# A mixture-of-experts stage: first tiles prepared one expert ahead, extra rows gathered and turned once for up to four lots, VectorE's order and the record loads changed

## What is computed

```python
def expert_block(args):
    xb, e = args
    return (jax.nn.silu(xb @ exp_w1[e]) * (xb @ exp_w3[e])) @ exp_w2[e]
y_buf = lax.map(expert_block, (buf.reshape(n_blocks, MOE_BLOCK, d), block_expert))
y = y_buf.reshape(n_blocks * MOE_BLOCK, d)[dest] * gate_sorted[:, None].astype(h.dtype)
out = jnp.zeros((n_tok, d), h.dtype).at[tok_sorted].add(y)
```

## Time and profile before

| | |
|---|---|
| median of 3 executions | 3097.43 us (3096.23 to 3101.21) |
| profiled execution, its own time | 3096.11 us |
| its span | 3094.0 us |
| TensorE matmul busy | 2624.5 us (85%) |
| VectorE, ScalarE busy | 1299.9 us (42%), 1085.1 us (35%) |
| expert stage, first turning to last output product | 2160.2 to 3078.3 us |

### The profile page before, as it was taken

The page is one execution under the profiler, slowest core; times in us unless marked ns, Lnnn a source line. Parts: engine busy times, 40 slices in busy tenths (PEclk is TensorE's granted clock), DMA queues, the critical chain, the costliest instruction groups (busy, mean ns, idle before and its releaser), DMA issues. The chain is left out here.

```text
span 3094.0 us, 40387 instructions
## 1 busy us (share of the span) xinstructions
PE 2624.5 (85%) x12691; PEld 1750.5 (57%) x12692; DVE 1299.9 (42%) x2250; ACT 1085.1 (35%) x2054; POOL 680.2 (22%) x1351
## 2 busy tenths in 40 slices
PE   5879999999677959768999999970988898886997
PEld 1326444444445445447998899860655565554664
DVE  5634671221122314132344554420746565453664
ACT  2542111111221211212344545410645565443563
POOL 2640110000000000006145555553122212222221
PEclk8989999999888979875799999965999999998999
DMA  5972211110499696761011111103886798765793
GB/s 183 330 212 72 52 45 31 52 55 28 129 245 222 149 233 156 175 186 34 29 58 54 54 54 58 58 35 124 312 286 208 246 330 286 233 205 181 239 351 113
DMA packets 307937, 472.00 MB, mean 153 GB/s; under 512 B 26852, under 2 KB 195180, under 8 KB 300996
## 3 DMA queue, kind: packets, MB, share of 16 engines
q1 hardware_dynamic: 229815, 396.89, 40.3%
q0 software_dynamic: 18416, 44.58, 6.3%
q10 hardware_dynamic: 59616, 29.38, 3.5%
HBM read 370.64 MB, written 108.05 MB: 155 GB/s over the span
## 5 line engine op out<-in xcount | busy, mean ns | idle before, releaser
L798 PE MATMUL ps_proj<-sb_hT,sb_win 128*128 128x512 f32 x768 | 336.1, 597 | 7.6 <-DVE sb_rot L903 6.0
L798 PEld LDWEIGHTS ps_proj<-sb_hT,sb_win 128*128 128x128 f32 x768 | 145.7, 192 | 189.9 <-issue 183.0
L2191 PE MATMUL ps_byp<-sb_w,sb_gT 128*128 128x512 f32 x512 | 236.0, 604 | 3.9 <-ACT sb_gT L2006 3.9
L1917 DVE TENSOR_TENSOR sb_w1l<-sb_raw,sb_w1h 128x1024 fp32r<-128x1024 f32 x128 | 148.2, 1220 | 167.8 <-ACT sb_w1h L1978 167.8
L1407 POOL MEMSET sb_pr<- 128x1026 int32 x1 | 1.0, 958 | 907.7 <-POOLq L186 907.7
L1686 DVE CUSTOM_DVE_ANT_0 sb_pr<-ps_S,sb_mask 128x640 f32<-128x640 f32 x128 | 105.6, 825 | 216.8 <-PE ps_S L1535 216.6
L1204 DVE TENSOR_TENSOR sb_ab<-sb_ab,ps_prod 128x512 f32<-128x512 f32 x64 | 44.1, 689 | 356.1 <-ACT sb_ab L1180 356.1
L1555 PE MATMUL ps_O<-sb_v,sb_pt 128*128 128x64 f32 (+1 forms) x1280 | 176.0, 293 | 0.0
L1555 PEld LDWEIGHTS ps_O<-sb_v,sb_pt 128*128 128x128 f32 x1280 | 173.3, 214 | 0.0
L1614 ACT COPY sb_pt<-ps_PT 128x512 f32<-128x512 f32 x128 | 74.6, 583 | 275.5 <-PE ps_PT L1541 275.4
L1917 DVE TENSOR_TENSOR sb_w3l<-sb_raw,sb_w3h 128x1024 fp32r<-128x1024 f32 x128 | 150.5, 1217 | 0.7 <-ACT sb_w3h L1978 0.5
(11 more groups left out here) (291 smaller groups left out, 5658.3 us busy)
## 6 DMA issues: line engine op xcount, KB each, us to landing
sb_raw<-in_exp_w SPq DMA_DIRECT2D x64, 2048.0 KB, 17.5
sb_w<-in_exp_w SPq DMA_DIRECT2D x32, 2048.0 KB, 9.1
sb_ada<-in_ada_w SPq DMA_DIRECT2D x16, 1536.0 KB, 8.1
scr_filt<-sb_fout ACTq DMA_DIRECT2D x128, 128.0 KB, 4.5
sb_yh<-scr_filt SPq DMA_DIRECT2D x32, 512.0 KB, 11.2
scr_hy_y<-sb_sp SPq DMA_DIRECT2D x32, 512.0 KB
sb_yx<-scr_hy_y SPq DMA_DIRECT2D x32, 512.0 KB, 7.9
scr_hy_v<-sb_yx SPq DMA_DIRECT2D x64, 256.0 KB, 4.3
```

What stands on the lines that cost most here:

```text
L798: ins = pe.matmul(mp[:, (NQ + n) % 4, :], w[:, pc % 3, k, (ct % 2) * P:(ct % 2 + 1) * P], g.hT[:, k, c * 512:(c + 1) * 512], start=(k == 0 ...
L1917: ve.tensor_tensor(piece(low[m], part), piece(raw13[par][:, m], part), piece(high[m], part).bitcast(F32), ALU.subtract).then_inc(lo[m], 1)
L2191: ins = pe.matmul(yp[:, part, :], gT[:, f, :], w2[par][:, f, part * 512:(part + 1) * 512], start=(f == 0), stop=(f == FT - 1), skip_group_ ...
```

## The change

An expert's first lots and its main tile are now prepared during the expert ahead of it. All rows from 129 to 256 of an expert are gathered once (buffer xgx), turned once in 8 transposes between the two halves of the hidden products of the expert before (function ahead), and scaled into xfx, from which up to four lots take their 32 columns. The four lots are four copies of the lot's code, each inside a condition on r, the number of these lots; rows beyond 256 go through a second loop (far) with four more copies. Lots and main tiles have semaphores of their own. VectorE computes two of the four low parts of w1 before the gated product and two after it, and three of w3's after the output scaling; ScalarE no longer casts a part of w3 ahead of the gated copies. The records of all experts are loaded at the start of the stage by 18 transfers that ScalarE issues, two over 128 partitions and 16 over 32; each 8-byte record is an element of its own in them. SyncE loads only weights. TensorE waits, ahead of turning xg, for the first low part of the next w1.

```diff
@@ -1776,9 +1776,10 @@
     GR = P // LOT
     FQ = 2 * FH // GR
     DQ = D // GR
-    MANY = 1 + (T - P) // LOT
-    TILES = NE + 2 * T // LOT
-    SLOTS = TILES + MANY + 4
+    NL4 = P // LOT
+    LOTS = 2 * T // LOT
+    FAR = LOTS // NL4
+    R, FURTHER, LOTS_AT, GROUP_AT, FAR_AT = range(5)
...
-        rec = e.sb(st, "brec", [P, SLOTS, 2], I32)
...
+        rec = e.sb(st, "brec", [P, NE, 2], I32)
+        recx = e.sb(st, "lot_rows", [P, NE, 2], I32)
+        recl = e.sb(st, "lot_records", [P, NE, NL4, 2], I32)
...
+        xgx = e.sb(st, "xg_lots", [P, D])
+        xfx = e.sb(st, "bxf_lots", [P, KT, P])
...
-        def span(eng, ex):
-            many = eng.value_load(info[0:1, 0, bass.ds(ex, 1)], min_val=1, max_val=MANY)
-            lots = eng.value_load(info[0:1, 1, bass.ds(ex, 1)], min_val=0, max_val=TILES - NE)
-            return many, lots
-
-        def experts(eng, lot, main):
-            def one(ex, par, half, last):
-                many, lots = span(eng, ex)
-                with eng.If(many > 1):
-                    with eng.Fori(0, many - 1) as b:
-                        lot(lots + ex + b, lots + b, ex, par, half)
-                main(lots + ex + many - 1, ex, par, half, last, lots + many - 1)
+        def column(eng, which, ex, least, most):
+            return eng.value_load(info[0:1, which, bass.ds(ex, 1)], min_val=least, max_val=most)
+
+        def experts(eng, ahead, lot, far, main):
+            def one(ex, par, half, r, last):
+                def lots(x, j):
+                    lot(x + j, j, recl[:, bass.ds(ex, 1), j, :].rearrange("p a b -> p (a b)"), ex, par, half)
+                    if j + 1 < NL4:
+                        with eng.If(r > j + 1):
+                            lots(x, j + 1)
+                with eng.If(r > 0):
+                    x = column(eng, LOTS_AT, ex, 0, LOTS)
+                    lots(x, 0)
+                    further = column(eng, FURTHER, ex, 0, T // P - 1)
+                    with eng.If(further > 0):
+                        at = column(eng, FAR_AT, ex, 0, FAR)
+                        with eng.Fori(0, further) as f:
+                            far(at + f, ex, r, f)
+                            for j in range(NL4):
+                                lot(x + r + NL4 * f + j, j, recfl[:, j, :], ex, par, half)
+                after = None if last else column(eng, R, ex + 1, 0, NL4)
+                main(ex, par, half, last, after)
+                return after
             eng.wait_ge(cnt, 1)
+            first = column(eng, R, 0, 0, NL4)
+            ahead(0, first)
             with eng.Fori(0, NE // 2 - 1) as pair:
-                one(2 * pair, 0, pair, False)
-                one(2 * pair + 1, 1, pair, False)
-            one(NE - 2, 0, NE // 2 - 1, False)
-            one(NE - 1, 1, NE // 2 - 1, True)
-            return eng.value_load(info[0:1, 2, NE - 1:NE], min_val=0, max_val=TILES - NE) + NE
+                after = one(2 * pair, 0, pair, column(eng, R, 2 * pair, 0, NL4), False)
+                one(2 * pair + 1, 1, pair, after, False)
+            after = one(NE - 2, 0, NE // 2 - 1, column(eng, R, NE - 2, 0, NL4), False)
+            one(NE - 1, 1, NE // 2 - 1, after, True)
...
+        rows_of = g.table[0:NE * CAP, :].rearrange("(e t) c -> t e c", e=NE)
+        records = [(rec[:, :, :], rows_of[0:P]), (recx[:, :, :], rows_of[P:2 * P])]
+        for q in range(GR):
+            for j in range(NL4):
+                records.append((recl[q * LOT:(q + 1) * LOT, :, j, :], rows_of[P + j * LOT:P + (j + 1) * LOT]))
...
+            def ahead(ex, r):
+                with ve.If(r > 0):
+                    group = column(ve, GROUP_AT, ex, 0, NE)
+                    ve.wait_ge(ttx, group + 2)
+                    ve.sem_inc(passed_v, 1)
+                    scale_rows(xfx).then_inc(xx_v, 1)
...
-            def main(n, ex, par, half, last, lots):
...
+            def main(ex, par, half, last, after):
                 if not last:
-                    weights_low(ex + 1, 1 - par, 0, range(PARTS))
+                    ahead(ex + 1, after)
+                    weights_low(ex + 1, 1 - par, 0, (0, 1))
                 ve.wait_ge(sgd, ex + 1)
                 ve.wait_ge(hm[1], ex + 1)
                 for c in range(FT):
                     cs = slice(c * P, (c + 1) * P)
                     ve.tensor_tensor(sg[:, cs], sg[:, cs], hp[:, 1, cs], ALU.mult).then_inc(gd, 1)
-                scaled(n + 1)
                 if not last:
+                    scaled(ex + 1)
+                    weights_low(ex + 1, 1 - par, 0, (2,))
+                    rows_low(ex + 1)
+                    weights_low(ex + 1, 1 - par, 0, (3,))
                     weights_low(ex + 1, 1 - par, 1, (0,))
-                rows_low(n + 1)
-                if not last:
-                    weights_low(ex + 1, 1 - par, 1, range(1, PARTS))
-                ve.wait_ge(added, n + 1)
+                ve.wait_ge(added, ex + 1)
                 for part in range(2):
                     cs = slice(part * 512, (part + 1) * 512)
                     ve.wait_ge(ym, 2 * ex + part + 1)
-                    ins = ve.scalar_tensor_tensor(out=y[:, cs], in0=yp[:, part, :], scalar=gate(n), in1=g2[:, cs],
+                    ins = ve.scalar_tensor_tensor(out=y[:, cs], in0=yp[:, part, :], scalar=gate(ex), in1=g2[:, cs],
                                                   op0=ALU.mult, op1=ALU.mult)
                 ins.then_inc(y_ok, 1)
+                if not last:
+                    weights_low(ex + 1, 1 - par, 1, range(1, PARTS))
 
             scaled(0)
             rows_low(0)
             weights_low(0, 0, 0, range(PARTS))
             weights_low(0, 0, 1, range(PARTS))
             ve.wait_ge(ld, 16 * (1 + GR))
-            experts(ve, lot, main)
+            ve.wait_ge(rl, 16 * (len(records) - 1))
+            experts(ve, ahead, lot, far, main)
...
+            def main(ex, par, half, last, after):
                 def gated_copied(c):
                     act.wait_ge(gtt, 4 * ex + c + 1)
                     act.copy(gT[:, c, :], gp[:, c % 2, 0:P]).then_inc(gtc, 1)
                 act.wait_ge(hm[0], ex + 1)
                 act.activation(sg[:, :], hp[:, 0, :], ACT.Silu).then_inc(sgd, 1)
                 if not last:
+                    ahead(ex + 1, after)
                     weights_high(ex + 1, 1 - par, half + par, 0, range(PARTS))
-                act.wait_ge(hm[1], ex + 1)
-                if not last:
-                    weights_high(ex + 1, 1 - par, half + par, 1, (0,))
                 gated_copied(0)
                 gated_copied(1)
-                scaled(n + 1)
+                if not last:
+                    scaled(ex + 1)
                 gated_copied(2)
                 gated_copied(3)
-                rows_high(n + 1)
                 if not last:
-                    weights_high(ex + 1, 1 - par, half + par, 1, range(1, PARTS))
-
+                    rows_high(ex + 1)
+                    weights_high(ex + 1, 1 - par, half + par, 1, range(PARTS))
+
+            for c, (dst, src) in enumerate(records):
+                act.dma_start(dst, src).then_inc(rl if c else rl0, 16)
             scaled(0)
             rows_high(0)
             for m in range(2):
...
+            def gather(ex):
+                if not (isinstance(ex, int) and ex == 0):
+                    pool.wait_ge(tt, ex)
+                    pool.sem_inc(passed, 1)
+                gathered(xg, picked_in, gat, rec[:, bass.ds(ex, 1), 0:1].rearrange("p a b -> p (a b)"), 0, ex)
+
+            def gather_ahead(ex):
+                with pool.If(column(pool, R, ex, 0, NL4) > 0):
+                    group = column(pool, GROUP_AT, ex, 0, NE)
+                    pool.wait_ge(ttx, group + 1)
+                    pool.sem_inc(passed, 1)
+                    gathered(xgx, picked_x, gatx, recx[:, bass.ds(ex, 1), 0:1].rearrange("p a b -> p (a b)"), 1, group)
+
+            def ahead(ex, r):
+                gather_ahead(0)
+                gather(1)
+                gather_ahead(1)
+
...
+            def main(ex, par, half, last, after):
+                if not isinstance(ex, int):
+                    gather_ahead(ex + 2)
+                    gather(ex + 2)
+                pool.wait_ge(y_ok, ex + 2)
...
+            pool.wait_ge(rl0, 16)
             gather(0)
-            gather(1)
-            total = experts(pool, lot, main)
-            pool.wait_ge(scat, 16 * total)
-            pool.wait_ge(gat, 16 * (total + 2))
-            pool.sem_inc(passed, 1)
+            pool.wait_ge(rl, 16 * (len(records) - 1))
+            pool.sem_inc(ttx, 1)
+            experts(pool, ahead, lot, far, main)
...
-            def records(ex):
-                many, lots = span(sp, ex)
-                with sp.If(many > 1):
-                    with sp.Fori(0, many - 1) as b:
-                        sp.wait_ge(rl, 16 * (lots + ex + b + 1))
```

(48 more changed lines are left out.)

199 lines of the change are left out of this document (119 added, 80 removed).

## The result

The changed kernel takes 3344.56 us (median of 4 runs, 3338.85 to 3350.23) against 3099.32 us for the kernel before in the same runs: ratio 1.0787, 95% interval 1.0759 to 1.0816. It is 7.9% slower, where 1.0% was forecast.

A forecast was written before the change was run, and what follows sets the result against it. TensorE was taken to bound experts without lots, with excess time in experts with lots. 3096.1 - 55.8 - 6.2 - 15.5 + 26 + 84 = 3128.6, given as 3129 us, 1.0% slower; 8-in-10 range 3037 to 3162.

The forecast's parts named there:

- Instructions: TensorE's two long branches after the last lot in 14 experts each wait 3.0 us for code: 84 us cost.
- the start: Stage start: ScalarE held issuing 24,576 record elements, and the first lot waits behind VectorE's subtractions; 26 us cost, 8 to 55.
- GpSimd: GpSimd's chain of adds and gather takes less than an expert, and its code has slack; cost nothing.
- Rival (d): Every long TensorE branch waits, in experts without lots too: 3156 us, or 3170 at 3.5 us a fetch; chance 0.08.
- Lots: Experts with lots: changed lots need no gather or turning in between, 7.6 us each in odd experts; 55.8 us saved.
- Rival (e): Lots don't get shorter, something else holds them: 30 us more, 3159 us with fetches, 3075 without; chance 0.05.
- VectorE's order: Gated product starts sooner with two low parts ahead of it: 0.5 us for each of 31 experts, 15.5 us saved.
- Records' waits and late weights: Without SyncE's waits for records, weights go out some 2.5 us earlier and late weights vanish: 6.2 us saved.

The follow-up runs named there:

- compact_turned: Changed kernel with lots in a loop, one code copy per engine, lot columns copied first, and records from one load turned on TensorE; 3051.35 us, 0.9866.
- unused17: Kernel before with seventeen never-entered copies of a lot's code added on TensorE; 3107.78 us, 1.0033.
- no_far_pool: Changed kernel with the never-entered code for rows beyond 256 left out on GpSimd alone; 3301.40 us, 1.0638.
- compact: Changed kernel with lots in a loop, one code copy per engine, lot columns copied first, keeping its 18 record loads; 3098.93 us, 1.0010.
- order_only: Kernel before with VectorE's new order alone; 3089.40 us, 0.9984.
- no_far: Changed kernel with the never-entered code for rows beyond 256 left out on TensorE, VectorE, ScalarE and GpSimd; 3199.84 us, 1.0306.
- unused2: Kernel before with two never-entered copies of a lot's code added on TensorE; 3167.35 us, 1.0240.
- unused1: Kernel before with one never-entered copy of a lot's code added on TensorE; 3098.77 us, 1.0011.
- records: Changed kernel with its sixteen lot-record loads replaced by sixteen copies within SBUF; 3326.92 us, 1.0717.
- turned: Changed kernel with all records made from one load of 32 pieces of 2 KB, turned on TensorE; 3302.38 us, 1.0664.

## Why the prediction was wrong

The direction came out right. The sum failed in three terms: the fetch of instructions, which step "Instructions" priced at 84 us, the start, put at 26 us, and GpSimd, whose chain was costed at nothing. The terms of the gain were nearly right in size.

- **Instructions, the failing step.** The mechanism was right, and so was the count: two long branches for each expert with lots, and 13 + 14 = 27 of them were long where 28 were counted. The price was not: 6.6 us at L1884 and 6.3 at L1890, where 3.0 were taken from small transfers and a packet's duration. The small transfers of rows 10 ran with the DMA engines about half busy; L1884's branch shown above ran with them at 1.00, and its packet starts only 4.1 us after it. (With them less than 60% busy a long branch takes 3.3 to 4.5 us, so even there 3.0 was low.) At the measured prices the 27 make 174 us where 84 were put. 14 others were long, 5 at L1886 and 9 at the loop's end, 59 us in all. Rival (d) had those in and ahead of experts without lots, which are 8. TensorE had products under way during 9 of the 14 and was idle behind the other 5 for 17 us together, so as a cost they are small. (At 3.5 us for a fetch, (d) itself adds up to 3174 and not 3170.) The lower clock behind a gap (22 us) was in no rival. Against compact_turned, where hardly a branch waits, the 13 experts with lots take 179.6 us more.
- **Which code stays.** The prediction said that 1,009 records stay and 3,700 are too many. This held, but not as a matter of length: 8,226 can be nearly free and 1,686 dear. What the Trainium skill, Runtime: NRT & Kernel Launch, section Instruction fetch mechanics, says of TensorE (2048 instructions, in blocks of 256) agrees with the eight blocks of the replay, with ten kernels beside it. It also says first in, first out, which the replay uses and no run here sets apart from dropping the block unused longest. The section's two-page window does not agree: in unused17, 11 of 14 branches over 3,710 instructions did not wait.
- **GpSimd.** "The other engines have a tenth of the code and more slack; I cost theirs at nothing." The part of the code was right (about 395 of its instructions for a pair, a tenth of TensorE's), the slack was not: its chain of one expert has no room for 4 to 5 us more. no_far_pool shows 46 us for it, mostly in the experts without lots, in which 51.6 us were lost where 15 were to be gained (6.2, and 18 times 0.5). Of the 51.6, 33 went with GpSimd's waits (417.6 against 384.4); the other 18 stayed, and TensorE's own long branches are among them.
- **The start.** The mechanism was right (ScalarE is held by the number of elements), and 74 us were the upper end. Its issues took 67 us in all (0.5 + 20.5 + 46.1), 2.7 ns for each of 24,576 elements, where 45 us were taken. The first issue took 0.5 us and the second, of the same size, 20.5: it is the loads ahead that hold the engine. What was missed is that the lots' gather waits for the last of the records, and that the first load lands late by itself: 62.5 us instead of 26, beyond the upper end of 55. compact against compact_turned gives 45 us for the loads.
- **Lots.** Saved 55.8 us by the prediction. In compact_turned the same experts save 50.2, of which some 5 are VectorE's order (511.5 against 506.5 in order_only), after 14.4 us paid for the copies of columns. In odd experts the next lot follows after 7.4 us in the changed kernel (7.6 predicted); in the two even experts with two lots it follows after 12.3 and 12.8 (11.4 predicted, with the table reloads). Rival (e) did not come.
- **VectorE's order.** 15.5 us by the prediction, 5 by order_only: 0.4 us an expert where 0.5 was taken, and some of it given back in experts that wait for something else.
- **Records' waits and late weights.** 6.2 us by the prediction; compact_turned's experts without lots save 3.2, with the order's share inside, so this term gave about nothing: one of them (expert 30) takes 25.4 us, against 21.8 before. That was not followed further.

What stays open: why the L1890 branches take 6.6 to 7.0 us also where the DMA engines are only 64 to 79% busy (7 of 14), which block TensorE drops, and how GpSimd's own store is laid out. With about 395 instructions for a pair it waits once an expert, with about 225 and 245 (no_far and compact) never.

## What to carry to other kernels

Code that isn't executed isn't free. Before unrolling something with few rounds, look at the page's instruction queues in a loop and count each engine's instructions, GpSimd's too; keep one copy in a loop and pay for a small copy of the operand instead. And where a table is wanted element by element across partitions, load contiguous rows and turn them on TensorE: 12 transposes and nine small copies took the place of 18 loads that cost 45 us.

## What the hardware showed that was not expected

- A taken branch into code that isn't there takes TensorE 3.3 to 4.5 us with the DMA engines less than 60% busy and 6.0 to 7.9 us with them 95% busy or more (33 of the 41 in the changed kernel; the other 8 lie between in DMA share and took 4.1 to 7.0).
- It is not a matter of length: 1, 2, 4, 8 and 17 unused copies cost 0.1, 2.4, 0.6, 2.6 and 0.3%. The 436 instructions that unused2 has more than unused1, never executed, moved the time by 2.3%.
- A stall takes more than itself: in the one shown the granted clock was 0.66 over the gap, 0.80 over the next 7 us, 1.00 after.
- A load of 4096 pieces of 8 bytes landed after 31 us and a second one after 43 while weights were loading (records); the 32 pieces of 2 KB held ScalarE for 0.4 us and landed after 3.7 (turned).
